# Retention query and key projections of one layer moved into a row of units of seven half-size products

## What is computed

```python
def odd_mixer(h_ctx, h_lat, w_in, w_out, cos, sin, need_ctx):
    ...
    p = split_parts(h_lat @ w_in, ODD_PARTS)
    names = [n for n, _ in ODD_PARTS] if need_ctx else ['k', 'v']
    pc = project_parts(h_ctx, w_in, ODD_PARTS, names)
    ...
    q_l = apply_rope(to_heads(p['q'], RET_HEADS).astype(F32), cos, sin)
    k_l = apply_rope(to_heads(p['k'], RET_HEADS).astype(F32), cos, sin) * k_scale
    v_l = to_heads(p['v'], RET_HEADS).astype(F32)
    ...
    y_lat = gated_head_norm(o_fw + flip(o_bw), p['g']).astype(dt) @ w_out
```

## Time and profile before

| what | us |
|---|---|
| median of three runs | 2555.9 |
| the three runs | 2553.59, 2556.48, 2555.9 |
| span of the profiled execution | 2552.4 |
| PE busy in that span | 2481.8 (97%) |
| DVE busy | 1672.4 (66%) |
| ACT busy | 657.5 (26%) |
| POOL busy | 73.0 (3%) |
| the row of units, first product to drain | 802.6 to 956.8 |
| queries and keys | 956.8 to 1042.7 |
| scores, weighting, products with the values | 1042.7 to 1084.0 |

### The profile page before, as it was taken

The page is one execution under the profiler, slowest core; times in us unless marked ns, Lnnn a source line. Parts: engine busy times, 40 slices in busy tenths (PEclk is TensorE's granted clock), DMA queues, the critical chain, the costliest instruction groups (busy, mean ns, idle before and its releaser), DMA issues.

```text
span 2552.4 us, 41132 instructions
## 1 busy us (share of the span) xinstructions
PE 2481.8 (97%) x16726; PEld 2005.8 (79%) x16726; DVE 1672.4 (66%) x3298; ACT 657.5 (26%) x1760; POOL 73.0 (3%) x96
## 2 busy tenths in 40 slices
PE   6999899999999999999999999999999999999999
PEld 3545458888888886599996867869997877868999
DVE  4967767655777645466673787657773777647785
ACT  3145512111101111122212153333321135333320
POOL 0000000000000001000000001100000000110000
PEclk9999999999999999999999999999999999999999
DMA  8532115555575868245544424135654344125563
GB/s 341 187 118 48 44 34 182 154 177 167 188 272 184 289 209 322 71 130 152 169 163 149 165 73 127 68 119 143 172 170 145 132 124 108 68 87 146 166 178 120
DMA packets 342651, 386.78 MB, mean 152 GB/s; under 512 B 8110, under 2 KB 285190, under 8 KB 330176
## 3 DMA queue, kind: packets, MB, share of 16 engines
q1 hardware_dynamic: 330896, 320.89, 40.1%
q0 software_dynamic: 8832, 57.26, 6.4%
q10 hardware_dynamic: 2736, 6.01, 0.6%
HBM read 383.08 MB, written 1.05 MB: 150 GB/s over the span
## 4 chain that ended last, share of the span: by engine, by line
PE 84%; DVE 9%; issue 3%; ACT 3%; DMA 2%; ACTq 0%; DVEq 0%; SPq 0%
PE acc L1032 33%; PE mx L1032 14%; PE acc L1083 10%; PE acc L1071 9%; PE acc L1093 5%; PE acc L1589 2%; PE acc L1538 1%; PE mx L1947 1%; DVE arena L3905 1%; PE mx L1398 1%; DVE hT L2894 1%; PE mx L1934 1%; PE mx L2006 1%; PE mx L1422 1%; DMA ring<-in_mod_w 0%
## 5 line engine op out<-in xcount | busy, mean ns | idle before, releaser
L1032 PE MATMUL acc<-arena 128*128 128x128 f32 (+1 forms) x2248 | 353.8, 300 | 1.0 <-ACT gate L2507 0.5
L1032 PEld LDWEIGHTS acc<-arena 128*128 128x128 f32 x2248 | 310.0, 192 | 16.8 <-ACT gate L2507 0.9
L2862 DVE SCALAR_TENSOR_TENSOR arena<-mod_w,vcols,arena 128x2048 f32<-128x2048 f32 x98 | 228.4, 2348 | 61.2 <-DMA mod_w<-in_w_ada 46.0
L1083 PE MATMUL acc<-hT,ring 128*128 128x256 f32 (+1 forms) x1024 | 249.8, 406 | 0.8 <-DVE arena L3579 0.8
L1083 PEld LDWEIGHTS acc<-hT,ring 128*128 128x128 f32 x1024 | 194.1, 190 | 54.1 <-issue 29.4
L1032 PE MATMUL acc<-hT,ring 128*128 128x128 f32 (+1 forms) x1368 | 206.1, 301 | 2.8 <-ACT hT L2255 1.4
L3255 DVE TENSOR_TENSOR arena<-ring 128x512 f32<-128x512 f32 (+1 forms) x136 | 91.7, 674 | 178.3 <-PE acc L1032 173.8
L1032 PEld LDWEIGHTS acc<-hT,ring 128*128 128x128 f32 x1368 | 184.8, 191 | 16.1 <-issue 6.4
L1071 PE MATMUL acc<-ring,hT 128*128 128x512 f32 x448 | 194.1, 593 | 2.2 <-ACT hT L2164 1.3
L1032 PE MATMUL acc<-arena,ring 128*128 128x128 f32 (+1 forms) x1256 | 194.2, 298 | 0.0
L1032 PEld LDWEIGHTS acc<-arena,ring 128*128 128x128 f32 x1256 | 171.1, 192 | 7.7 <-issue 0.8
(11 more groups left out here) (543 smaller groups left out, 3857.4 us busy)
## 6 DMA issues: line engine op xcount, KB each, us to landing
ring<-in_w_in SPq DMA_DIRECT2D x28, 2048.0 KB
mod_w<-in_w_ada POOLq DMA_DIRECT2D x48, 1024.0 KB, 5.5
ring<-in_ffn_w_in SPq DMA_DIRECT2D x88, 512.0 KB
ring<-in_w_up SPq DMA_DIRECT2D x88, 512.0 KB
mod_w<-in_mod_w SPq DMA_DIRECT2D x36, 1024.0 KB, 5.0
ring<-in_odd_w_in SPq DMA_DIRECT2D x20, 1024.0 KB
ring<-in_ffn_w_out SPq DMA_DIRECT2D x16, 1024.0 KB
ring<-in_w_down SPq DMA_DIRECT2D x16, 1024.0 KB
```

Source lines behind the costliest of these rows:

```text
L1032: ins = nc.tensor.matmul(out, w[:, k, :], h[:, k, :], start=start and k == 0, stop=stop and k == n - 1, skip_group_check=more)
L1083: ins = nc.tensor.matmul(b[:, 0:hi - lo], w[:, k, P * f:P * (f + 1)], hT[:, k, lo:hi], start=k == 0, stop=k == KD - 1)
L2862: ins = V.scalar_tensor_tensor(acc_, mod_w[:, i % 2, :], vcols[:, at:at + 1], acc_, ALU.mult, ALU.add)
```

## The change

Queries and keys become eight more units of the same row, two per tile, numbers 12 to 19 (`RV_UNITS`, tiles 8 and 9 for queries, 10 and 11 for keys). In these the weights are the stationary operand: a query unit makes 256 columns for 256 latent tokens with products of 128 tokens each, a key unit 256 columns for all 512 tokens with products of 256. Product 2 stands directly behind product 1 in them. t4 overwrites a weight block in the ring, so the loads of tiles 10 and 11 wait for product 3 of the last unit of tiles 8 and 9. Sums of tokens of both pairs now lie side by side (`gate`, `arena`), one sum in place in `hT`. The slabs are spread anew (`MOD_UNITS`); the gates' SiLU goes to units 13 to 16 on ACT; two of the four rotations go behind the last two units' sums, before `c10` of unit 19.

```diff
-MOD_SUM_AFTER = {"even": (13,), "odd": (1, 4, 8, 20, 25)}
+MOD_SUM_AFTER = {"even": (13,), "odd": (1, 4, 8, 15, 18)}
-MOD_UNITS, MOD_ODD = (1, 2, 3, 2, 3, 2, 3, 2, 0, 0, 0, 0), 14
+MOD_UNITS = (1, 2, 3, 2, 3, 2, 3, 2, 1, 1, 1, 1, 1, 0, 1, 0, 3, 3, 2, 0)
 RV_UNITS = [(c, pair) for c in range(4) for pair in range(2)] + [(c, 1) for c in range(4, 8)]
-RV_TILES = 8
+RV_UNITS += [(c, part) for c in range(8, 12) for part in range(2)]
+RV_TILES, RQ_TILE, RK_TILE = 12, 8, 10
...
+            if c == RK_TILE:
+                return [x[:, 0, 4 * j:4 * j + 4, :] for j in range(2)]
+            return [view(19456 + 1024 * j, 4, 256) for j in range(2)]
...
+                    elif c - 2 >= RQ_TILE:
+                        sp.wait_ge(rv_z, rv_last(c - 2))
                     elif c >= 2 and half == 0:
...
+                    if tile_of(q) >= RQ_TILE:
+                        product2(q)
                     product5(q)
                     product4(q - 1)
                     product6(q)
-                    product2(q)
+                    if tile_of(q) < RQ_TILE:
+                        product2(q)
                     product3(q - 1)
                     mod_after("odd")
                     product7(q)
...
             retention_values(2)
-            for lo in (256, 256, 0, 0):
-                by_feature(4, lo, 512, where="odd")
-            pe.wait_ge(mod_c, len(MOD_GROUPS))
...
+                if q == 13:
+                    silu_tanh()
+                if 13 <= q < 17:
+                    act.wait_ge(rv_c10, q - 4)
+                    for t in range(2):
+                        g = rg[:, t, 512 * (q - 13):512 * (q - 12)]
+                        nc.scalar.activation(g, g, ACT.Silu)
...
+                    elif c == RK_TILE + 1:
+                        dve.wait_ge(mod_red, len(MOD_GROUPS) - 2)
                     dve.wait_ge(w_in[t // 2 % RING], pl.landed[t][1])
...
+                c = RV_UNITS[q][0] if q < units else RV_TILES
+                ends = q < units and q == rv_last(c) - 1
+                if ends and c < RQ_TILE:
+                    value_weights_summed(c + 1, (0, 1, 2) if c + 1 < RQ_TILE else (0, 1))
+                if q < units:
+                    dve.wait_ge(rv_p2, q + 1)
+                    dve.wait_ge(rv_p1s, q + 1)
+                    V.tensor_tensor(rv_out(q, 0, 0), rv_bank(5, q), rv_copy(q, 0), ALU.add).then_inc(rv_c00, 1)
+                    if ends and c >= RQ_TILE:
+                        value_weights_summed(c, (2,))
+                        if c + 1 < RV_TILES:
+                            value_weights_summed(c + 1, (0, 1))
+                    mod_slabs(MOD_UNITS[q])
+                if units - 1 <= q <= units:
+                    turned(q - units + 1)
+
+            turned(RET - 2)
```

More of the change, by code:

```diff
@@ L385, in make_plan @@
     a.start("ret_v")
-    for c in range(8):
-        a.ring_used("unit", rv_last(c), 2)
-    tiles("odd", (("ret_q", [4, 4]), ("ret_k", [4, 4])))
+    for c in range(RV_TILES):
+        a.ring_used("unit" if c < RQ_TILE else "wide", rv_last(c), 2)
     a.free_jobs("ret_oT", KD)
@@ L590, in ff_sums @@
             return [v.rearrange("p (k t) -> p k t", t=w) for v in flat]
[L592 to L596, removed]
-        def rv_weight_sums(c):
-            return [view(12288 + 3072 * (c % 2) + 1024 * j, 4, 256) for j in range(3)]
+        rv_s1, rv_s2, rv_s4 = (v.rearrange("p (k r n) -> p k r n", k=4, r=2) for v in (
+            gate[:, 0, :], view(18432, 1024), gate[:, 1, :]))
@@ new lines, in first_then_second_block, with rv_pairs, rv_tokens, rv_token_sum @@
+        by_pair = hT[:, :, :].rearrange("p (k e) (r i n) -> p k e r i n", e=2, r=2, i=2)
+        def rv_pairs(q):
+            c, part = RV_UNITS[q]
+            return part if c < RQ_TILE else 1 if c < RK_TILE else slice(0, 2)
+        def rv_tokens(q, i, e):
+            return by_pair[:, :, e, rv_pairs(q), i, :]
+        def rv_token_sum(q, s):
+            return rv_tokens(q, 1, 0) if s == 3 else (rv_s1, rv_s2, None, rv_s4)[s - 1][:, :, rv_pairs(q), :]
+        def rv_features(q, w):
+            c, part = RV_UNITS[q]
+            return w if c < RQ_TILE else w[:, :, P * part:P * (part + 1)]
@@ L1836, in retention_values, with times @@
                 fresh[0] = None
-                h = by_parity(hT)
-                A = [[[h[:, :, e, 256 * pair + P * i:256 * pair + P * (i + 1)] for e in range(2)] for i in range(2)]
-                     for pair in range(2)]
                 B = {}
                 units = len(RV_UNITS)
+                def times(out, q, tokens, w, start, stop, ready=lambda k: None):
+                    w = rv_features(q, w)
+                    pair_ = (tokens, w) if RV_UNITS[q][0] < RQ_TILE else (w, tokens)
+                    return product(rv_bank(out, q), *pair_, start, stop, ready, more=not start)
@@ L2588, in _ @@
                         act.wait_ge(rv_c10, q - 1)
-                    nc.scalar.activation(u2[:, b], seven(b, 256), ACT.Copy).then_inc(rv_u2s, 1)
+                    nc.scalar.activation(rv_copy(q, 1), rv_bank(q % 2, q), ACT.Copy).then_inc(rv_u2s, 1)
+                    if q == units - 1:
+                        table(0)
                 if q >= 1:
@@ L2595, in _ @@
                         act.wait_ge(rv_c11, q - 1)
-                    nc.scalar.activation(u3[:, b], seven(b, 256), ACT.Copy).then_inc(rv_u3s, 1)
-            silu_tanh()
-            table(0)
-            table(1)
[L2600 to L2608, removed]
+                    nc.scalar.activation(rv_copy(q, 2), rv_bank(q % 2, q), ACT.Copy).then_inc(rv_u3s, 1)
+                if q == 13:
[5 more added lines that the diff above has]
+                        nc.scalar.activation(g, g, ACT.Silu)
+            table(1)
             exp_ln()
-            for f in range(8):
-                evac(rk[:, f, :], 512)
-                mod_after("odd")
             for h in range(RET):
@@ L3522, in value_weights_summed @@
             def value_weights_summed(c, only=(0, 1, 2)):
-                t3, t2, t4 = rv_weight_sums(c)
+                t3, t2, *rest = rv_weight_sums(c)
                 t = pl.tile["ret_v"] + 2 * c
@@ L3603, in turned @@
                 dve.wait_ge(ret_rope, h + 1)
-            for h in range(RET - 1):
-                turned(h)
+            units = len(RV_UNITS)
+            for q in range(units + 2):
+                if 1 <= q < units + 1:
+                    o = q - 1
+                    dve.wait_ge(rv_u3s, o + 1)
+                    V.tensor_tensor(rv_out(o, 1, 1), rv_bank(2 + o % 3, o), rv_copy(o, 2), ALU.add).then_inc(rv_c11, 1)
+                if q >= 2:
+                    o = q - 2
+                    dve.wait_ge(rv_z, o + 1)
+                    V.tensor_tensor(rv_out(o, 1, 0), rv_bank(2 + o % 3, o), rv_copy(o, 1), ALU.add).then_inc(rv_c10, 1)
+                c = RV_UNITS[q][0] if q < units else RV_TILES
[14 more added lines that the diff above has]
+            turned(RET - 2)
             def weighted(h):
```

127 lines of the change are left out of this document (66 added, 61 removed).

## The result

The changed kernel takes 2560.9 us (median of 9 runs, 2559.4 to 2561.7), the kernel before beside it 2554.5 us (9 runs, 2552.6 to 2556.6). The ratio is 1.0026, with a 95% interval of 1.0017 to 1.0035: **slower by 6.4 us**. The forecast was 2559.1 us, with a range of 2551 to 2566. Run again, the ratio was 1.0032 (1.0020 to 1.0044).

A forecast was written before the change was run, and what follows sets the result against it. The stretch was taken to be bound by PE's own products, with slack on DVE and DMA. Savings of -9.2 us and added waits summed to +3.2 us, on the median 2559.1 us, range 2551.0 to 2565.7.

The forecast's parts named there:

- the clock: Rival, 0.05: the row's three new gaps of 3 to 4 us halve PE's clock; 17 us, half of that added, 2567.
- products: In the row's query and key units, smaller products at 7/8 of the work replace 82.6 us: -9.2 us.
- tile 7: A slab per unit in units 8 to 11 delays this tile and its sums: +0.5 us, between 0 and 1.2.
- `c00` of unit 11: Product 2 of unit 12 waits for this quarter behind three sums of tile 8: +3.0 us, between 1.4 and 4.0.
- tile 10: Its load starts late, shares engines with a slab; product 1 of unit 16 waits: +3.8 us, between 0.6 and 5.9.
- `c11` of unit 17: Product 3 of unit 17 waits behind tile 11's sums and three slabs: +3.0 us, between 0.3 and 5.7.
- row's end, scores, weighting: After unit 18, rotations on DVE delay `c10` of unit 19 (+0.7 us) and the first weighting (+1.1 us).
- restarts: Each of four restarts of PE after a wait costs 0.1 us: +0.3 us.
- its high ends: All upper bounds of the added waits taken together: +9.8 us.
- the first rival: Tiles 8 and 10 land in 5.1 and 7.7 us, tile 11 meets one slab: -4.9 us; chance 0.13.
- Second rival: Slabs running through the row delay tiles 10 and 11 to 13 and 15.6 us: +8 us, 2564; chance 0.33.
- the prediction's own sign of being wrong: Wrong if granted clock leaves 1.00 in this stretch, tiles 8, 10, 11 land unnoticed, or query units exceed 6.3 us.

The follow-up runs named there:

- the combined kernel: Changed kernel, t4 of tile 8 apart, two slabs of unit 17 early, first two rotations before `c10` of unit 18, product 2 late in unit 12: ratio 0.9961.
- the spare products: Changed kernel plus nine unread matmuls in the waits before product 1 of unit 16 and product 3 of unit 17: ratio 1.0019, again 1.0012.
- product 2 late: Changed kernel with product 2 behind product 6 in the query and key units too: one time, 2559.3 us beside 2554.2 for the kernel before.
- rotations: Changed kernel with the first two rotations before `c10` of unit 18, the third behind the first weighting: one run, 2557.8 us beside 2552.8.
- new slabs: Changed kernel with only the table of slabs changed, none in units 12 to 15: ratio 1.0018 to the kernel before.

## Why the prediction was right or wrong

The time was close (1.8 us) and the range held it, but the likeliest case was "within 0.2%", and it is slower by a little more: +6.4 us on the kernel before, where +3.2 was forecast. The waits came where they were named; one step failed, the clock.

A wait costs PE more than its idle time: where the row ended in the kernel before, 0.47 us idle cost 2.37 - 1.73 = 0.64 before and 1.83 - 1.73 = 0.10 behind, 0.27 in addition. With that, forecast and stage compare, in us:

| term | forecast | measured |
|---|---|---|
| products | -9.2 | -9.3 |
| tile 7 | +0.5 | +1.7 |
| `c00` of unit 11 | +3.0 | +1.7 |
| tile 9 | 0 | +0.7 |
| tile 10 | +3.8 | +5.2 |
| `c11` of unit 17 | +3.0 | +4.1 |
| row's end, scores, weighting | +1.8 | +2.2 |
| restarts | +0.3 | in the above |
| clock | 0 | +4.6 |
| sum | +3.2 | +10.9 |

The products are what is left of the 10.9 us when the rest is taken off; the combined kernel, with hardly a wait, gives -9 as well. Two sums of the prediction are 0.1 us off: its products give -9.3, its high ends +9.9.

- *Products*: right. 128 tokens run at 0.89 us (970.13 to 971.02), 256 at 1.73 (1030.06 to 1031.79). In units 13 to 16, where ACT makes the SiLU pairs, PE waits for nothing of ACT's.
- *Tile 7*: named, but past its high end of 1.2 us: PE waits 0.65 us for the tile and 0.47 for its sum b, with 0.27 in addition to each.
- *c00 of unit 11*: mechanism right, term mis-sized. The second half of tile 8 was issued at 944.25 and its first sum starts at 949.40: 5.15 us, the low end, as the first rival had it, where I took 6.5.
- *Tile 10*: mechanism right, 1.4 us more, inside its bounds. 12.2 us from the end of product 3 of unit 13 (forecast 10.9), PE there after 7.3 (7.1). With no slab beside it, it took 8.0 us from issue to use (forecast 7.7), with one 12.05. That a slab from POOL's queue and a tile from SP's share the engines, as the Trainium skill has it ("DMA: Bandwidth & Descriptors", section "Issuing engines are not separate DMA queues"), shows in these 4 us.
- *c11 of unit 17*: right in each step, 1.1 us more in all: done 27.8 us after product 3 of unit 15 (27.0), PE there after 24.1 (24.0), tile 11 used 13.8 us after its issue at 996.96 (13), the third slab landing 5.05 us after its own (5.1).
- *Second rival* (slabs push further): half of it. It put 13 us for tile 10 and 15.6 for tile 11, between which and the forecast the 12.2 and 13.8 us lie.
- *Row's end*: right in its sum; the waits stand at the scores (1.49 us for `c10`, 1.24 for the weighting). The scores start at 1049.62, forecast 1044 to 1046, by all that came before.
- *The clock*: **the step that failed.** "The granted clock reads 1.00 even around the first", and so 0.05. That reading lies at the program's start, and the trace itself speaks against it there. The weight loads of the first long product behind the 14.77 us, in groups of four:

```profile
17.40 0.19 PEld L1301 LDWEIGHTS mx<-ring,cond 128*32 128x32 f32 x4 [0.66 <-issue]
...
18.25 0.19 PEld L1301 LDWEIGHTS mx<-ring,cond 128*32 128x32 f32 x4 [0.66 <-issue]
...
20.20 0.12 PEld L1301 LDWEIGHTS mx<-ring,cond 128*32 128x32 f32 x4 [0.31 <-issue]
20.63 0.12 PEld L1301 LDWEIGHTS mx<-ring,cond 128*32 128x32 f32 x4 [0.31 <-issue]
```

  Equal groups follow at a pitch of 0.85 us first and of 0.43 from 19.77 us on, which is what half and full clock would give, while the windows read 1.00 from 0 to 25 us. So this reading was no evidence that idle time leaves the clock alone. Further on, the same trace does read lower values, which the prediction leaves out. A wait of PE, and windows:

```profile
281.56 0.63 PE L1559 MATMUL mx<-fconst,arena 128*128 128x128 f32 x4 [1.87 <-ACT arena L2432]
```

```profile
282.00:284.00 2.00, 2.00 (x7) 0.60 0.03 8
...
310.00:312.00 2.00, 2.00 (x25) 0.50 0.08 31
```

  They stand in a stage of short products with waits of up to 1.87 us. That the granted clock leaves 1.00 in the stretch of the change was the prediction's own sign of being wrong, and it came. The rival had the mechanism and doubled products; it priced 17 us and halved that, measured are 4.6. The Trainium skill's warning ("TensorE: Matmul & The Clock Gate", section "Why this matters for your kernels": an idle gap between bursts can put the clock back to half) holds here, and the spare products show it.

That the time still came out near is luck. The stage lost 7.7 us more than forecast: 4.6 by the clock, the rest by waits that were some tenths to 1.4 us longer than priced, with `c00` shorter. Against that, the medians differ by 4.5 us less than the profiled stages do, and the kernel before took 2554.5 us in nine runs where the forecast had started from 2555.9 in three: 7.7 - 4.5 - 1.4 is the 1.8 us. The forecast was right on where PE waits, short on what the waits cost, and lucky on the total.

## What to carry to other kernels

Seven eighths of the work is a gain only if the loads keep pace: units half as long leave half the time for a tile of the same size, so follow each load from the read that frees its place. Price a wait with what comes behind it: idle time, restart and, for the long ones, products at half clock. Work that has two buffers and takes longer to load than to do, as the slabs here (5.05 us to land, 2.4 to read), stalls at the third in a row; put it where its engine waits anyway.

## What was not expected of the hardware

Which wait brings the clock down doesn't follow from its length alone. In this stage the eight waits of 3.43 to 4.93 us (six profiles) were all followed by a granted clock of 0.5, and none up to 1.66 us. In between it differs: 2.78 us (product 2 late) and 3.20 us twice (changed kernel's second profile, rotations) were, 2.99, 3.00 and 3.20 us (spare products' second profile, new slabs) were not. The same length goes both ways in the kernel before: of two waits of 1.87 us, at 234.22 and 281.56 us, only the second was followed by a lower clock. What it costs differs too: behind 4.77 to 4.93 us, the four products from product 1 of unit 16 on took 7.8 to 9.1 us in four profiles, against 6.2 at 2.4 GHz. What decides stays open.
